# A two-layer retention, delta-rule and memory decoder: memory operands and gate columns laid out anew, and the loop over layers written out

## The chip, the cores and the metric

The kernel runs on one core of one Trainium2 chip. The metric is device time in microseconds (us) for one launch, as the median of several runs. One more execution is recorded by the hardware profiler, and all durations below come from that one. The engines are PE (matrix products; PEld is its weight load), DVE (vector), ACT (scalar functions), POOL (here it issues DMAs) and SP (it issues the weight DMAs).

## The reference

Two decoder layers run over 256 prompt tokens and 8 sample tokens, 264 columns in all, in float32. Per layer:

```
h = x + 1/2 * post(SwiGLU_1(pre(x)))                               D_MODEL 1024, D_FF 2816
h = h + post(W_out( sum_i sigmoid(gate_i) * W_branch_i(branch_i(pre(h))) ))
h = h + 1/2 * post(SwiGLU_2(pre(h)))
branches: retention (4 heads), gated delta rule (4 heads), cross-attention into 256 memory rows
memory keys and values:  mem_k = rms_norm(mem, norm_mem[l]) @ w_mem_k[l],  the same for mem_v
gated delta rule:        a, b = 8 columns of xn @ w_in;  g = -exp(a_log) * softplus(a + dt_bias);  beta = sigmoid(b)
```

Only the gain `norm_mem[l]` differs between the layers in the input of the memory products; the 256 memory rows themselves are the same. The post norms need sums of squares over the features.

## The kernel before, in words

**Layout and precision.** Activations lie transposed: features on the 128 partitions, in 8 tiles, and the 264 tokens as columns. Every large product is made of three products in the 32-bit reduced format (fp32r): high part times high part, input low part times weight high part, input high part times weight low part. So each chunk of weights that arrives in `raw` (two slots of 2048 columns, up to 1 MB each) is split by ACT into its high part (`wh`, L1178) and by DVE into the remainder (`wl`, L1596). Small products (sums of squares over partitions, transposes, decays, the 8 gate columns) are full float32 products, which the chip runs as two records of matmul each.

**Stages.** The table `PHASES` gives the order of the weight groups of a layer: mvb (memory values, second half), f1i and f1o (first SwiGLU), mk (memory keys), mq, rqk, rv (queries, retention), gq, x2, rg, x0, gz, g1 (delta rule, and the branches with their gates), b1 (delta branch's output), out, mva (memory values of the next layer, first half), f2i, f2o (second SwiGLU). A group is 48 matmuls on PE (33 in f1o and f2o). While PE is in group n, SP loads group n+2 or n+3, and ACT and DVE split group n+2. The small work of the branches hangs between the groups, written by hand: functions `after`, `mid` and `inner` on PE, and their counterparts on ACT and DVE. Each engine runs its own program; semaphores alone tie them, and within an engine the order is the written one.

**The loop over layers.** Every engine holds one copy of a layer inside `Fori(0, L)` with L = 2, and the layer number `l` is a register. A wait for "the nth use in layer l" is then a register sum followed by a wait. Inside it the long stages f1i, f1o, f2i and f2o are inner loops of four groups a turn.

**The memory rows.** The prologue makes the transposed, normalised rows in `y`, scales them by the first layer's gain into `memh` (ACT, L1252) and `meml` (DVE, L1688), and stores the unscaled rows to DRAM (`mem_t`, 1 MB). `memh` and `meml` share their place with the hidden units and with `old` of the delta branch, so they are made anew in every layer: POOL loads the rows into `mnt` (L531) after `o_gdn`, ACT scales them after group 0 of stage out, and DVE makes four of eight remainders after group 0 and four after group 1 of out. Stage out is followed by the total `p2` (L648), by mva and by the norm of the residual (`n3`, L641).

**The gates.** `gab` multiplies the 8 tiles of `y` as the stationary side by 64 columns of `wab` as the moving side, 24 float32 products, after group 2 of mq (L732). Its 8 useful columns per token tile become `gb`. In x2, after group 0, `gcol` makes four products of 4 columns (L923, L924) and `gev` eight of 8 columns (L930). In x0, after group 3, `gmt` sums squares by eight products of 8 columns (L1074).

## Time and profile before

| what | value |
|---|---|
| median of 3 runs | 2129.01 us (2123.88 to 2131.65) |
| profiled execution, its own time | 2127.21 us |
| its span, first to last instruction | 2125.6 us |
| PE busy | 1990.0 us, 94% of the span, 15638 matmuls |
| DVE, ACT busy | 1325.7 us (62%), 911.0 us (43%) |
| DMA | 370.94 MB, mean 175 GB/s |
| chain that ended last | PE 74%, DVE 15%, issue 6%, ACT 3%, DMA 1% |

The profiled execution is 1.8 us under the median and inside the range of the runs. A busy PE is not a PE at its peak, because matmuls overlap; the time from one start to the next tells what one costs. The chain is followed back from the last instruction through whatever released each step, so an engine's share of it is what sets the end, and "issue" is time in which the engine waited for nothing that the profile shows.

### The profile page before, as it was taken

The numbers are of one execution on the slowest core, as the hardware profiler recorded it, in microseconds if no ns is written. First come the engines' busy times: TensorE is split into PE (matmuls) and PEld (weight loads), VectorE is DVE, ScalarE is ACT, GpSimd is POOL, SyncE is SP. The second block draws the span as 40 slices with busy tenths as digits, with TensorE's granted clock in tenths as the row PEclk, the third lists the DMA queues.
The fourth block names the chain that finished last, engine by engine and source line by source line (L and its number), as shares of the span: only waits on it lengthen the run. The fifth ranks groups of instructions, "written<-read, shape, count | busy, mean of one in ns | idle before, by whom it ended". The sixth has DMA issues, their size and how long they took to land.

```text
span 2125.6 us, 42629 instructions
## 1 busy us (share of the span) xinstructions
PE 1990.0 (94%) x15638; PEld 1937.2 (91%) x15638; DVE 1325.7 (62%) x1996; ACT 911.0 (43%) x997; POOL 118.2 (6%) x173
## 2 busy tenths in 40 slices
PE   4999999999998999899989999999999899989997
PEld 3999989899987998899989998988999899979997
DVE  3655576647547767756566556675664767776556
ACT  2444345324553454444344434452355343444433
POOL 1000001001110101000000000010111000000000
PEclk8999999999999999999999999999999999999998
DMA  6665657545653546466656655664556345536654
GB/s 214 179 178 167 189 165 224 165 155 189 216 175 100 183 154 231 140 183 177 169 159 181 182 168 159 205 222 140 188 193 208 119 141 187 179 120 178 179 165 151
DMA packets 437539, 370.94 MB, mean 175 GB/s; under 512 B 9427, under 2 KB 415317, under 8 KB 437011
## 3 DMA queue, kind: packets, MB, share of 16 engines
q1 hardware_dynamic: 413520, 280.86, 44.4%
q0 software_dynamic: 23856, 87.98, 12.5%
q8 instruction: 95, 1.56, 0.3%
q14 instruction: 68, 0.55, 0.1%
HBM read 343.16 MB, written 25.64 MB: 173 GB/s over the span
## 4 chain that ended last, share of the span: by engine, by line
PE 74%; DVE 15%; issue 6%; ACT 3%; DMA 1%; DVEq 1%; SPq 0%; ACTq 0%
PE proj L607 47%; PE proj L630 4%; PE proj L625 4%; PE proj L626 4%; PE proj L605 2%; PE aux L817 2%; DVE wl L1596 1%; PE aux L657 1%; PE aux L902 1%; DVE y L1735 1%; PE aux L1029 1%; DVE c_t L2044 1%; DVE t_t L2138 1%; DVE qkvt L1907 1%; PE aux L748 1%
## 5 line engine op out<-in xcount | busy, mean ns | idle before, releaser
L1596 DVE TENSOR_TENSOR wl<-raw,wh 128x2048 fp32r<-128x2048 f32 (+1 forms) x284 | 608.3, 2142 | 196.1 <-ACT wh L1178 170.9
L1178 ACT CAST wh<-raw 128x2048 fp32r<-128x2048 f32 (+1 forms) x284 | 507.5, 1787 | 429.1 <-PE proj L607 263.7
L607 PE MATMUL proj<-xh,wh 128*128 128x264 f32 x2688 | 418.8, 293 | 4.7 <-ACTq L1270 4.5
L607 PE MATMUL proj<-xl,wh 128*128 128x264 f32 x2688 | 419.6, 291 | 1.4 <-DVEq L1708 1.4
L607 PE MATMUL proj<-xh,wl 128*128 128x264 f32 x2688 | 406.1, 288 | 3.7 <-DVE wl L1596 3.6
L607 PEld LDWEIGHTS proj<-xh,wh 128*128 128x128 f32 x2688 | 357.6, 190 | 11.7 <-ACTq L1270 5.0
L607 PEld LDWEIGHTS proj<-xl,wh 128*128 128x128 f32 x2688 | 361.6, 191 | 2.7 <-DVEq L1708 2.6
L607 PEld LDWEIGHTS proj<-xh,wl 128*128 128x128 f32 x2688 | 356.2, 190 | 5.4 <-DVE wl L1596 5.4
L626 PE MATMUL proj<-hl,wh 128*128 128x264 f32 x704 | 174.5, 284 | 0.0
L625 PE MATMUL proj<-hh,wh 128*128 128x264 f32 x704 | 174.4, 285 | 0.0
L626 PEld LDWEIGHTS proj<-hl,wh 128*128 128x128 f32 x704 | 132.7, 188 | 0.0
L625 PEld LDWEIGHTS proj<-hh,wh 128*128 128x128 f32 x704 | 132.5, 188 | 0.0
L1630 DVE TENSOR_TENSOR tmpf<-proj,gate 128x264 f32<-128x264 f32 x88 | 38.1, 432 | 141.4 <-PE proj L607 141.4
L817 PE MATMUL aux<-pv,sring 128*128 128x64 f32 x512 | 86.4, 250 | 12.1 <-DVEq L360 12.1
L630 PE MATMUL proj<-hh,wl 128*128 128x264 f32 x704 | 96.4, 285 | 0.0
L817 PEld LDWEIGHTS aux<-pv,sring 128*128 128x128 f32 x512 | 80.6, 192 | 13.8 <-DVEq L360 10.8
L1216 ACT ACTIVATE gate<-proj 128x264 f32<-128x264 f32 x120 | 47.0, 392 | 102.4 <-PE proj L607 101.4
L630 PEld LDWEIGHTS proj<-hh,wl 128*128 128x128 f32 x704 | 90.3, 188 | 0.0
L1245 ACT ACTIVATE sqt<-proj 128x264 f32<-128x264 f32 x48 | 18.8, 392 | 111.1 <-PE proj L630 82.2
L1383 ACT COPY full<-proj 128x256 f32<-128x256 f32 x32 | 12.0, 374 | 126.3 <-PE proj L607 126.3
L1646 DVE TENSOR_SCALAR y<-proj,gl 128x264 f32 (+1 forms) x48 | 23.6, 492 | 57.4 <-ACTq L1246 53.8
L1789 DVE CUSTOM_DVE_ANT_0 junk<-sring,aux 128x256 f32<-128x256 f32 x128 | 46.4, 417 | 14.3 <-PE aux L705 4.8
(389 smaller groups left out, 2574.7 us busy)
## 6 DMA issues: line engine op xcount, KB each, us to landing
raw<-ffn_w_in SPq DMA_DIRECT2D x176, 512.0 KB, 4.8
raw<-w_in SPq DMA_DIRECT2D x80, 1024.0 KB, 5.5
raw<-ffn_w_out SPq DMA_DIRECT2D x64, 704.0 KB, 4.5
sring<-cache_mem_k POOLq DMA_DIRECT2D x32, 512.0 KB, 5.1
sring<-cache_mem_v POOLq DMA_DIRECT2D x32, 512.0 KB, 3.9
out<-sring POOLq DMA_DIRECT2D x32, 512.0 KB, 4.5
sring<-state_gdn POOLq DMA_DIRECT2D x32, 512.0 KB, 4.9
raw<-w_mem_v SPq DMA_DIRECT2D x12, 1024.0 KB, 5.2
```

Source lines behind the costliest of these rows:

```text
L605: mm = pe.matmul(o, a[:, k, t * P:(t + 1) * P], w[:, s, k * 256:(k + 1) * 256], **go)
L607: mm = pe.matmul(o, w[:, s, k * 256 + t * P:k * 256 + (t + 1) * P], a[:, k, :], **go)
L625: pe.matmul(o, w, high[:, kk, :], start=(kk == 0), stop=False)
L626: pe.matmul(o, w, low[:, kk, :], start=False, stop=False)
L630: mm = pe.matmul(o, wl[:, s, k * P:(k + 1) * P], high[:, kk, :], start=False, stop=(kk == FT - 1))
L817: mm = pe.matmul(values.o[:, 0, k * WIDE:(k + 1) * WIDE], sring[:, values.slot, k * P:(k + 1) * P], pv[:, col:col + WIDE], start=True, sto ...
L1178: act.copy(wh[:, slot, 0:size], raw[:, slot, 0:size]).then_inc(hi_done[slot], 1)
L1216: order(act.activation(gate[:, slot, :], proj[bank][:, 0:T], func))
L1596: dve.tensor_sub(wl[:, slot, 0:size], raw[:, slot, 0:size], wh[:, slot, 0:size].bitcast(F32)).then_inc(split_done[slot], 1)
L1630: order(tt(tmpf[:], proj[bank][:, 0:T], gate[:, u % 2, :], ALU.mult))
L1646: order(ts_(y[:, j, :], proj[bank][:, 0:T], gl[:, j, gain:gain + 1], None, ALU.mult))
L1789: order.apart(dve.tensor_tensor_reduce(junk[:, z, :], sring[:, slot, z * 256:(z + 1) * 256], o[:, 0, z // 2 * 256:(z // 2 + 1) * 256], 1.0 ...
```

## The change

Four things are changed.

1. **Memory operands.** The prologue makes high and low parts for both layers, the second pair in `saveh` and `savel`, and stores that pair to DRAM (`next_h`, `next_l`, 2 MB). In each layer POOL loads both straight into `memh` and `meml` (2 MB) once ACT tells `b1_done`, in group 0 of out. The scaling by ACT and DVE in stage out is gone, and so are `mnt` and `gmem`. PE waits for the load ahead of mva.
2. **Gate columns.** `wab` is split by DVE into high and low parts (`wabr`, 40 columns: 8, a gap, 8). It is now the stationary side: 16 fp32r products with 264 moving columns (`gaw`) after group 1 of mq. DVE copies the 40 rows to `tmpf`, and three float32 products against `sel` add the two halves and turn them (`gab`) after group 2.
3. **Wide products.** `gcol` is two products of 8 columns, `gev` one of 64 columns against a diagonal that DVE makes in `gus`, `gmt` two of 32 columns.
4. **The loop over layers** is a Python loop on all five engines: two copies of the layer in sequence, with waits on constants. The inner loops stay.

```diff
-            pool.wait_ge(pro_dve, 16)
-            pool.dma_start(mem_t, y[:, :, 0:NM]).then_inc(mem_saved, 16)
+            pool.wait_ge(M["mem_split"], 2)
+            pool.dma_start(next_h, saveh[:]).then_inc(mem_saved, 16)
+            pool.dma_start(next_l, savel[:]).then_inc(mem_saved, 16)
...
-            with pool.Fori(0, L) as l:          # the same on sync, tensor, scalar and vector
+            for l in range(L):
...
-                pool.wait_ge(mem_saved, 16)
-                pool.wait_ge(M["o_gdn"], l + 1)
+                pool.wait_ge(mem_saved, 32)
+                pool.wait_ge(M["b1_done"], l + 1)
                 passed(pool)
-                pool.dma_start(mnt[:], mem_t).then_inc(mem_loaded, 16)
+                pool.dma_start(memh[:], next_h).then_inc(mem_loaded, 16)
+                pool.dma_start(meml[:], next_l).then_inc(mem_loaded, 16)
...
                         if g == 1:
                             spread(0)
+                            ready("wab_split")
+                            o = begin(l, "gaw")
+                            for k in range(KT):
+                                pe.matmul(o[0:40, 0, 0:T], wabr[:, k, :], xh[:, k, :], start=(k == 0), stop=False)
+                            for k in range(KT):
+                                mm = pe.matmul(o[0:40, 0, 0:T], wabr[:, k, :], xl[:, k, :], start=False, stop=(k == KT - 1))
+                            end(mm, "gaw")
                     elif g == 2:
-                        pe.wait_ge(wab_loaded, 16 * (l + 1))
+                        ready("abx")
                         o = begin(l, "gab")
                         for t in range(3):
                             n = P if t < 2 else NS
-                            for k in range(KT):
-                                mm = pe.matmul(o[0:n, 0, t * WIDE:(t + 1) * WIDE], y[:, k, t * P:t * P + n], wab[:, 8 * k:8 * k + WIDE],
-                                               start=(k == 0), stop=(k == KT - 1))
+                            mm = pe.matmul(o[0:n, 0, t * 8:t * 8 + 8], tmpf[0:40, t * P:t * P + n], sel[0:40, :], start=True, stop=True)
...
-                        for c in range(2):
-                            pe.matmul(o[:, 0, c * 4:c * 4 + 4], tri[:], gb[:, c, 0:4], start=True, stop=True)
-                            mm = pe.matmul(o[:, 0, 8 + c * 4:12 + c * 4], ones[:], gb[:, c, 0:4], start=True, stop=True)
+                        pe.matmul(o[:, 0, 0:8].rearrange("p (c h) -> p c h", c=2), tri[:], gb[:, 0:2, 0:4], start=True, stop=True)
+                        mm = pe.matmul(o[:, 0, 8:16].rearrange("p (c h) -> p c h", c=2), ones[:], gb[:, 0:2, 0:4], start=True, stop=True)
...
-                        for h in range(H):
-                            for k in range(2):
-                                c = (k * H + h) * NS
-                                mm = pe.matmul(o[:, 0, c:c + NS], gb[0:NS, 2, k * H + h:k * H + h + 1].broadcast_to([NS, P]), ident[0:NS, 0:NS],
-                                               start=True, stop=True)
-                        end(mm, "gev")
+                        end(pe.matmul(o[:, 0, 0:2 * H * NS], ones[0:NS, :], gus[0:NS].rearrange("p c b -> p (c b)"), start=True, stop=True), "gev")
...
-                        for h in range(H):
-                            for dt in range(2):
-                                mm = pe.matmul(o[:, 0, h * NS:(h + 1) * NS], ones[:], csum[:, 2 * h + dt, :], start=(dt == 0), stop=(dt == 1))
+                        for dt in range(2):
+                            mm = pe.matmul(o[:, 0, 0:H * NS].rearrange("p (h b) -> p h b", b=NS), ones[:], csum[:, dt:KT:2, :],
+                                           start=(dt == 0), stop=(dt == 1))
...
-                pe.wait_ge(M["mem_split"], l + 2)
+                pe.wait_ge(mem_loaded, 32 * (l + 1))
                 products(l, "mva", memh, meml, "natural", groups=(0,))
...
-            scale_memory(0, y)
+            scale_memory(0, memh)
+            scale_memory(1, saveh)
...
-                def next_memory(g):
-                    if g == 0:
-                        act.wait_ge(mem_loaded, 16 * (l + 1))
-                        scale_memory((l + 1) % L, mnt)
-                stream(l, "out", squares(l), after=next_memory, hold=True)
+                stream(l, "out", squares(l), after=lambda g: tell("b1_done") if g == 0 else None, hold=True)
...
-            split_memory(1, y)
+            split_memory(0, memh, meml)
+            split_memory(1, saveh, savel)
             stream(0, "mv0")
-            dve.wait_ge(mem_saved, 16)
...
                 stream(l, "mvb", groups=(1,))
+                dve.wait_ge(mem_saved, 32)
                 stream(l, "f1i", hidden_tile(l, True))
...
+                dve.wait_ge(wab_loaded, 16 * (l + 1))
+                order(cp(wabr[:, :, 0:8], wab[:]))
+                order(tt(wabr[:, :, 32:40], wab[:], wabr[:, :, 0:8].bitcast(F32), ALU.subtract))
+                tell("wab_split")
...
+                    if g == 1:
+                        order(cp(tmpf[0:40], take(dve, l, "gaw")[0:40, 0, 0:T]))
+                        release(dve, "gaw")
+                        tell("abx")
...
+                        order(tt(gus[0:NS], gb[0:NS, 2, :].unsqueeze(2).broadcast_to([NS, 2 * H, NS]),
+                                 ident[0:NS, 0:NS].unsqueeze(1).broadcast_to([NS, 2 * H, NS]), ALU.mult))
...
-                order(cp(gmem[:], gains[:, :, bass.ds((l + 1) % L + 12, 1)]))
-                stream(l, "out", result_tile(l, 3, "sqp"), hold=True,
-                       late=lambda g: split_memory(l + 2, mnt, range(4 * g, 4 * g + 4)) if g < 2 else None)
+                stream(l, "out", result_tile(l, 3, "sqp"), hold=True)
```

Adding `gaw` to the list of small products moves the PSUM banks of the nine that follow it by one place; from `ms1` on the banks are as before.

On PE in stage mq, from the turn of the first memory keys on, the kernel before has (aux are the PSUM banks of the small products, proj those of the large ones; names in brackets are the semaphores waited for):

```order
L607 MATMUL proj<-xh,wh 128x264 [waits bank_free1]
L607 MATMUL proj<-xh,wh 128x264 x7
L607 MATMUL proj<-xl,wh 128x264 x8
L607 MATMUL proj<-xh,wl 128x264 x8
L727 REGISTER_ALU
L573 REGISTER_ALU [waits wab_loaded]
L732 MATMUL aux<-wab,y 128x64 [waits aux_free1]
L732 MATMUL aux<-wab,y 128x64 x15
L732 MATMUL aux<-wab,y 8x64 x8
L705 MATMUL aux<-qst,selr 128x256 [waits aux_free2]
```

The changed kernel has in the same stage, one group earlier and then at the same place:

```order
L707 MATMUL aux<-qst,selr 128x256
L731 MATMUL aux<-xh,wabr 40x264 [waits aux_free3,wab_split]
L731 MATMUL aux<-xh,wabr 40x264 x7
L733 MATMUL aux<-xl,wabr 40x264 x8
L609 MATMUL proj<-xh,wh 128x264 [waits bank_free0,hi_done0]
...
L609 MATMUL proj<-xh,wl 128x264 x8
L740 MATMUL aux<-sel,tmpf 128x8 [waits aux_free2,abx]
L740 MATMUL aux<-sel,tmpf 128x8
L740 MATMUL aux<-sel,tmpf 8x8
L707 MATMUL aux<-qst,selr 128x256 [waits aux_free3]
```

The 24 products after group 2 are replaced by 16 after group 1 and 3 after group 2, and the second lot waits for DVE (`abx`).

On DVE in stage out, groups 0 and 1, the kernel before has (meml are the low parts of the memory rows, wl those of the weights, acc the running sum of squares):

```order
L1596 TENSOR_TENSOR wl<-raw,wh 128x2048 [waits order_dve,hi_done0]
L1686 REGISTER_ALU
L1688 SCALAR_TENSOR_TENSOR meml<-mnt,gmem,memh 128x256 [waits memhi]
L1688 SCALAR_TENSOR_TENSOR meml<-mnt,gmem,memh 128x256 x3
L296 ISA [waits order_dve]
L1144 REGISTER_ALU
L1645 REGISTER_ALU [waits first_done]
L1646 TENSOR_SCALAR y<-proj,gl 128x264 [waits sq_ready]
L1647 TENSOR_TENSOR acc<-acc,sqt 128x264 [waits order_dve]
```

and the changed kernel:

```order
L1593 TENSOR_TENSOR wl<-raw,wh 128x2048 [waits order_dve,hi_done0]
L296 ISA
L1643 TENSOR_SCALAR y<-proj,gl 128x264 [waits sq_ready,first_done]
L1644 TENSOR_TENSOR acc<-acc,sqt 128x264 [waits order_dve]
L1643 TENSOR_SCALAR y<-proj,gl 128x264 [waits order_dve,sq_ready,group_done1]
```

The remainders are out of DVE's way, and so are the register sums ahead of each tile.

On PE at the end of the first layer the kernel before has (the branch back is at L662, the target is the first row of mvb):

```order
L648 MATMUL aux<-acc,ones 128x264 [waits aux_free0]
L662 REGISTER_ALU
L662 COMPARE_AND_BRANCH
```

and the changed kernel runs on:

```order
L650 MATMUL aux<-acc,ones 128x264 [waits aux_free0,sqp]
L607 MATMUL proj<-wh,memh 128x256 [waits bank_free0,hi_done0]
L607 MATMUL proj<-wh,memh 128x256 x7
L607 MATMUL proj<-wh,meml 128x256 x8
L607 MATMUL proj<-wl,memh 128x256 [waits split_done0]
```

The branch between the total `p3` and mvb is gone; what stands on both sides of it is the same.

## Rows read from the trace of the kernel before

**Rows 1.** Busy time by stretch: us, each engine's busy time, PEclk, DMA share, GB/s.
```profile
311.00:352.00 41.00, 41.00 (x302) 37.61 (x302) 26.52 (x77) 17.28 (x26) 5.99 (x8) 1.00 0.66 212
508.00:586.00 78.00, 76.25 (x615) 75.04 (x613) 48.14 (x88) 43.77 (x40) 12.45 (x17) 0.98 0.65 207
668.00:720.00 52.00, 48.18 (x406) 47.03 (x405) 36.09 (x49) 23.69 (x31) 3.77 (x5) 1.00 0.40 129
888.00:1016.00 128.00, 128.00 (x1060) 128.00 (x1059) 75.51 (x89) 56.00 (x49) 0.00 (x0) 1.00 0.63 175
848.00:850.00 2.00, 2.00 (x19) 2.00 (x18) 1.32 (x4) 2.00 (x2) 0.00 (x0) 1.00 1.03 403
864.00:866.00 2.00, 2.00 (x11) 1.95 (x10) 1.07 (x1) 1.46 (x2) 0.00 (x0) 0.50 0.99 261
```

**Rows 2.** Chain that ended last: start, length, engine, tile, line, count.
```profile
318.16 4.51 PE aux L732 x48
516.50 1.88 PE aux L930 x16
700.07 1.92 PE aux L1074 x16
```

**Rows 3.** Timeline of mq and x2: start, length, engine, line, operation, [idle before].
```profile
314.10 0.08 DVE L1789 DVE_READ_ACCUMULATOR2_ANT sall<- 128x1 f32 x1
515.49 0.34 PE L923 MATMUL aux<-gb,tri 128*128 128x4 f32 x2
```

**Rows 4.** Timeline of the end of out, both layers.
```profile
843.15 3.31 ACT L1252 ACTIVATE memh<-mnt,gains 128x256 fp32r<-128x256 f32 x8
845.89 8.04 SPq L424 DMA_DIRECT2D raw<-w_mem_v  x2
853.23 1.67 DVE L1688 SCALAR_TENSOR_TENSOR meml<-mnt,gmem,memh 128x256 fp32r<-128x256 f32 x4
853.82 1.91 ACT L1178 CAST wh<-raw 128x2048 fp32r<-128x2048 f32 x1 [1.11 <-DMA raw<-w_mem_v]
858.25 2.29 DVE L1596 TENSOR_TENSOR wl<-raw,wh 128x2048 fp32r<-128x2048 f32 x1 [0.62 <-DVE acc L1647]
863.01 1.25 PE L648 MATMUL aux<-acc,ones 128*128 128x264 f32 x2 [4.93 <-DVEq L1651]
876.00 1.80 DVE L1733 RECIPROCAL rt<-rt 128x264 f32<-128x264 f32 x1 [1.55 <-ACTq L1270]
1892.94 1.25 PE L648 MATMUL aux<-acc,ones 128*128 128x264 f32 x2 [4.90 <-DVEq L1651]
```

**Rows 5.** Timeline of the totals p1 and p3, and of the next layer's start.
```profile
267.27 0.71 PE L648 MATMUL aux<-acc,ones 128*128 128x264 f32 x2 [1.85 <-DVEq L1651]
279.72 1.80 DVE L1733 RECIPROCAL rt<-rt 128x264 f32<-128x264 f32 x1 [1.55 <-ACTq L1270]
1079.11 0.97 PE L648 MATMUL aux<-acc,ones 128*128 128x264 f32 x2 [1.84 <-DVEq L1651]
1083.57 2.07 PE L605 MATMUL proj<-wh,memh 128*128 128x256 f32 x8 [3.49 <-issue]
1096.87 1.80 DVE L1733 RECIPROCAL rt<-rt 128x264 f32<-128x264 f32 x1 [4.32 <-ACTq L1270]
```

**Rows 6.** Chain that ended last, in stage b1 of both layers.
```profile
806.89 6.87 DMA raw<-w_branch_gdn
1837.36 6.16 DMA raw<-w_branch_gdn
```

**Rows 7.** Timeline around b1 (first two rows) and of the prologue.
```profile
804.87 0.55 POOL L531 DMA_DIRECT2D mnt<-mem_t  x1 [35.46 <-issue]
815.73 2.29 DVE L1596 TENSOR_TENSOR wl<-raw,wh 128x2048 fp32r<-128x2048 f32 x1 [2.14 <-ACT wh L1178]
51.44 2.29 DVE L1596 TENSOR_TENSOR wl<-raw,wh 128x2048 fp32r<-128x2048 f32 x1 [10.31 <-ACT wh L1178]
```

**Rows 8.** Landing times of the DMAs issued at L424, min, median, max.
```profile
DMA to landing us min/median/max: 4.2/5.1/14.5
```

More of the change, by code:

```diff
@@ L96 @@
          + ["p2", "n3", "p3"])
-ONE_BANK = ("n1 n2 n3 p1 p2 p3 gab smt spt rks gcs rqd gcol gev gqd gkS gmt mqs0 mqs1 mqs2 mqs3 "
+ONE_BANK = ("n1 n2 n3 p1 p2 p3 gaw gab smt spt rks gcs rqd gcol gev gqd gkS gmt mqs0 mqs1 mqs2 mqs3 "
             + " ".join(f"{n}{k}" for n in ("sp", "rd", "gd") for k in range(2 * NS)) + " "
@@ L127, in build @@
     (t_ident, t_swap, t_tri, t_masks, t_rot, t_dec, t_kdec, t_sel) = tables
-    mem_t = nc.dram_tensor("mem_t", (P, KT, NM), F32).ap()
+    next_h, next_l = (nc.dram_tensor(n, (P, KT, NM), F32R).ap() for n in ("next_h", "next_l"))
     ctx = ExitStack()
@@ L194, in build @@
         sqw = at("sqw", 29184, [P, KT, T])
-        mnt = at("mnt", 16896, [P, KT, NM])
+        saveh, savel = at("saveh", 0, [P, KT, NM], F32R), at("savel", 8192, [P, KT, NM], F32R)
         xnat = at("xnat", 0, [P, 3, D])
@@ L428, in _ @@
                     load(0, 0, name, PLAN[name], 0, g)
-            with sp.Fori(0, L) as l:
+            for l in range(L):
                 for name, _, _ in PHASES[1:]:
@@ L485, in store_prompt_state @@
                 pool.dma_start(to[l, 0].rearrange("h k v -> k h v"), stg[:].rearrange("p (h v) -> p h v", h=H)).then_inc(done, 16)
-            with pool.Fori(0, L) as l:
+            for l in range(L):
                 passed(pool)
-                pool.dma_start(wab[:, 0:KT * 8].rearrange("p (k n) -> p k n", n=8), w_in[l].rearrange("(k p) n -> p k n", p=P)[:, :, C_AB:C_AB + 8]).then_inc(wab_loaded, 16)
+                pool.dma_start(wab[:], w_in[l].rearrange("(k p) n -> p k n", p=P)[:, :, C_AB:C_AB + 8]).then_inc(wab_loaded, 16)
                 for n in range(SRING):
@@ L661, in _ @@
             products(0, "mv0", memh, meml, "natural")
-            with pe.Fori(0, L) as l:
+            for l in range(L):
                 def ready(name):
@@ L1247, in squares, with scale_memory @@
                 return tile
-            def scale_memory(layer, src):
+            def scale_memory(layer, out):
                 for k in range(KT):
-                    order.apart(act.activation(memh[:, k, :], src[:, k, 0:NM], ACT.Copy, scale=gains[:, k, bass.ds(layer + 12, 1)]))
+                    order.apart(act.activation(out[:, k, :], y[:, k, 0:NM], ACT.Copy, scale=gains[:, k, layer + 12:layer + 13]))
                 order.wait()
@@ L1258, in _ @@
                 split(0, s, 0, GW)
-            scale_memory(0, y)
+            scale_memory(0, memh)
+            scale_memory(1, saveh)
             order.fresh()
             stream(0, "mv0", copied(0, lambda g, t: mvn[:, t, g * 256:(g + 1) * 256]))
-            with act.Fori(0, L) as l:
+            for l in range(L):
                 def ready(name):
@@ L1562, in _ @@
             order(dve.memset(qsm[:, H * NS:], 0.0))
-            order(dve.memset(wab[:, KT * 8:], 0.0))
+            order(dve.memset(wabr[:].bitcast(F32), 0.0))
             dve.sem_inc(pro_act, 1)
@@ L1588, in _ @@
             dve.sem_inc(pro_dve, 1)
-            order(cp(gmem[:], gains[:, :, 12:13]))
             dve.sem_inc(M["x_half"], 1)
@@ L1681, in merge_tile, with split_memory @@
                 return tile
-            def split_memory(n, src, tiles=range(KT)):
-                if 0 in tiles:
-                    dve.wait_ge(M["memhi"], n)
-                for k in tiles:
-                    order.apart(stt(meml[:, k, :], src[:, k, 0:NM], gmem[:, k, :], memh[:, k, :].bitcast(F32), ALU.mult, ALU.subtract))
+            def split_memory(layer, high, low):
+                dve.wait_ge(M["memhi"], layer + 1)
+                for k in range(KT):
+                    order.apart(stt(low[:, k, :], y[:, k, 0:NM], gains[:, k, layer + 12:layer + 13], high[:, k, :].bitcast(F32), ALU.mult, ALU.subtract))
                 order.wait()
-                if KT - 1 in tiles:
-                    dve.sem_inc(M["mem_split"], 1)
+                dve.sem_inc(M["mem_split"], 1)
             order.fresh()
@@ L1695, in _ @@
                 split(0, s, 0, GW)
-            split_memory(1, y)
+            split_memory(0, memh, meml)
+            split_memory(1, saveh, savel)
             stream(0, "mv0")
-            dve.wait_ge(mem_saved, 16)
             dve.wait_ge(M["stz"], 2)
-            with dve.Fori(0, L) as l:
+            for l in range(L):
                 def ready(name):
```

14 lines of the change are left out of this document (7 added, 7 removed).

## The prediction

> **What bounds the kernel now.** I read busy time by stretch first. In mq PE is busy for all of 41.00 us, in f2i for all of 128.00 us, in x2 for 76.25 of 78.00, in x0 for 48.18 of 52.00 [rows 1]. So in most of the program PE's instruction stream is the limit, and a record taken off PE is worth its distance to the next start. The f2i stretch gives the price of a large matmul: 1060 starts in 128.00 us, 0.121 us each [rows 1]. Then I read the chain that ended last: the small products that the change shrinks stand on it, 4.51 us for the gate columns, 1.88 us for `gev`, 1.92 us for `gmt` [rows 2]. The timeline then shows the places where PE stands still: 4.93 and 4.90 us ahead of the total p2 at the end of out, waiting for DVE, where p1 and p3 wait 1.85 and 1.84 us [rows 4, 5]; and 3.49 us at the start of the second layer, waiting for nothing that the profile shows [rows 5]. Last, in b1 the chain runs through a weight DMA of 6.87 us, 6.16 us in the second layer [rows 6].
>
> **The change part by part.** The sum is made against the profiled execution's 2127.2 us.
>
> *Small products, on PE.* Gate columns: 48 records go, 4.51 us [rows 2]. In come 16 products with 264 moving columns at 0.121 us [rows 1], 1.94 us, and three float32 products, 6 records at the 0.118 us of `gev` (1.88 / 16 [rows 2]), 0.7 us. Saved: 1.87 us. `gcol`: its 8 records run from 515.49 until `gev` at 516.50, 1.0 us [rows 2, 3]; half go, 0.5 us. `gev`: 16 records become 2, with 64 columns, which take 0.094 us in L732 (4.51 / 48): 1.88 - 0.19 = 1.69 us. `gmt`: 16 records at 0.12 us become 4: 1.44 us. A wider moving side has no row of its own at 32 columns; it lies between the 4 to 8 columns of `gcol` and `gev` and the 64 of L732, and none of these is above 0.13 us. Together 5.5 us per layer, 11.0 us for two. In mq and x2 nothing else is late and it counts in full. In x0 PE idles for 3.8 us of 52 because the inversion goes back and forth between PE, ACT and DVE [rows 1], so I let a third of `gmt`'s part drown there: 10.0 us. Bounds: 5 (half is absorbed) and 11.
>
> What DVE does in addition (two small operations for `wabr`, a copy of 40 rows, one product for `gus`) lies in stages where it is busy for 26.5 of 41 us and 48 of 78 us [rows 1], so I cost it at nothing. The new wait `abx` stands behind group 2 of mq on PE, with sample scores and the next group queued behind it. DVE's last score of that turn ended at 314.10 and PE came to the gate products at 318.16 [rows 2, 3]; the copy fits into those 4 us, and PE comes 1.9 us later than today. If it did not, the price would be the wait itself, at most 2 us a layer.
>
> *Stage out.* ACT loses 3.31 us of scaling and DVE two lots of 1.67 us [rows 4]. PE ended its last product at 863.01 - 4.93 = 858.08. DVE's last split ran from 858.25 to 860.54, and from there to p2 it took 2.47 us for the last two tiles. Without the remainders that split can start when ACT's weight cast ends, 853.82 + 1.91 = 855.73, since the tiles before it are then done; it ends at 858.0 and p2 starts at 860.5: 2.5 us earlier [rows 4]. What is late next is the weight DMA that ACT waits for (1.11 us). In the second layer I take the limit that p1 shows, 1.85 us behind PE's last product: 1892.94 - 4.90 + 1.85 = 1889.9, 3.0 us earlier [rows 4, 5]. Afterwards: from p2 to the reciprocal of the next norm today's kernel takes 876.00 - 863.01 = 12.99 us, from p1 279.72 - 267.27 = 12.45 us [rows 4, 5]; after the long idle the two matmuls of the total take 1.25 instead of 0.71 us and the stretch behind it has a granted clock of 0.50, the lower level of 1.2 GHz [rows 1, 4]. A shorter idle should leave the clock up: 0.5 us each. Together 5.5 + 1.1 = 6.6 us. Bounds: 0 (the load's traffic takes it, below) and 8.
>
> PE's new wait is for the 2 MB load, with mva, the sum n3 and all of f2i queued behind it. The load can be issued when ACT has cast the weights of group 0, at about 843.2, where the scaling began [rows 4]. At the 403 GB/s of the fullest stretch [rows 1] 2 MB need 5.2 us, at half of that, sharing with weights, 10.4: it lands by 856, before PE wants it at 860.5.
>
> *Start of the second layer.* From p3 to the reciprocal it takes 1096.87 - 1079.11 = 17.76 us, where the same work behind p1 takes 12.45 [rows 5]. The 3.49 us of waiting for nothing and the slow matmuls behind it (2.07 us for eight) are the difference. Both go when PE runs straight on: 5.3 us. Bounds: 3.5, the gap alone, and 5.8.
>
> *Stage b1.* Today's 1 MB load of `mnt` is issued at 804.87, next to the weight DMA of 806.89 that the chain waits for [rows 6, 7]. That DMA took 6.87 and 6.16 us, where the median of its kind is 5.1 [rows 8]. The load moves out of this stage, so 1.8 + 1.1 = 2.9 us. DVE stood idle for 2.14 us behind it in the first layer [rows 7], so there is room. Bounds: 0 (others share the queue) and 4.
>
> *Register sums.* With constants the register operations ahead of waits go. Where PE streams they cost nothing: 128.00 of 128.00 us busy with them [rows 1]. Between DVE tiles they may be worth a few hundredths each. I take 2 us, bounds 0 and 8.
>
> *Prologue.* Eight more scalings on ACT and eight on DVE, about 3.3 us on each, fall into a stretch where DVE idles 10.31 us behind ACT [rows 7], which itself waits for PE's first memory group: nothing. If that cover were gone it would be 3.3 us. The 2 MB store goes out later than today's 1 MB; DVE waits for it before f1i, some 25 us later.
>
> Sum: 10.0 + 6.6 + 5.3 + 2.9 + 2 = 26.8 us, 2127.2 - 26.8 = 2100.4 us. The median of the runs is 1.8 us above the profiled execution, so I forecast 2102 us.
>
> The Trainium skill has a rule on the third term: "Runtime: NRT & Kernel Launch", section "Instruction fetch mechanics", says that code is fetched ahead in sequence only, and that a taken branch to code outside the window at hand stalls the engine. The trace agrees at the start of the second layer (3.49 us) and not in the inner loops, whose branches back show no gap. By the rule the four inner loops would have something to give too; by the rows they have nothing, and they stay in any case.
>
> **The rivals.**
>
> *A, products gain less.* Stages mq, x2 and x0 turn out to be tied to DVE and ACT soon after PE gets faster. For it: x0's idle 3.8 us. Against: none in mq. The products give 3 instead of 10 and the register sums nothing: 2111 us.
>
> *B, the memory load collides.* From 843 on POOL has 2 MB of memory rows and 2 MB of sample keys to load, beside the weights of mva (845.89 [rows 4]), where DMA is full already (share 1.03 [rows 1]). If the memory rows, whose pieces are 8 KB, go ahead of the weights' 1 KB pieces, the weights come later by up to 2 MB / 403 GB/s = 5.2 us in the first layer, and every us of it is a us at p2, since ACT's cast, DVE's split and the last tiles follow each other. Then the first layer loses 5.2 - 2.5 = 2.7 us instead of gaining 3.0, and the second gains nothing: 2102 + 5.7 + 3.5 = 2111 us. If also the load itself ran at the slowest rate seen, 14.5 us for 1 MB [rows 8], it would land at 872, and PE would wait 11.7 us ahead of mva in each layer: 2125 us. For it: the 14.5. Against: that one stood behind POOL's whole first batch of loads in the prologue, and the load is first in POOL's queue.
>
> *C, slower: fetching the written-out code stalls PE.* Place: the inner loops. f1i and f2i turn five times, f1o and f2o three, so there are 12 branches back in a layer, 24 in all. Should they cost what the branch at the layer's end costs, 3.49 us, because the copies lie differently in memory: 24 x 3.49 = 84 us, 2186 us. It decides from 8 of the 24 on (26.8 / 3.49). Against: none of them costs anything now, and the bodies only get shorter.
>
> *D, writing out the layers is worth more.* If each engine answers faster wherever it waited on a register, the register term is 12 instead of 2: 2092 us. For it: "issue" is 6% of the chain. Against: most of that is between operations whose waits are constants already.
>
> **How the numbers follow.** Forecast 0.58 (range of its own 2094 to 2110), A 0.14, B 0.12, C 0.04, D 0.12. The range 2089 to 2119 leaves out C, the far end of B and the ends of D. A measurement of this kernel can tell 0.5%, 10.6 us, from no change, so faster means below 2118.4. That takes the forecast, A, D and most of B, less a tenth for what I haven't seen: 0.87. Same: 0.09. Slower: 0.04, C.
>
> **What would show it.** Right: p2 follows PE's last product of out by under 3 us and the reciprocal follows p2 by 12.5; no gap on PE between p3 and mvb, and 12.5 us to the reciprocal; L731 and L733 some 2 us together, stages mq and x2 2 us shorter each; the b1 weight DMA near 5 us. Wrong: PE waiting for `mem_loaded`, `abx` or `wab_split`; ACT's cast before the last tiles of out waiting for its DMA by several us; PE gaps without a releaser in f1i or f2i.

## The result and the profile after

The changed kernel takes 2107.01 us (median of 4 runs, 2103.46 to 2107.55), the kernel before 2129.04 us (4 runs, 2123.88 to 2131.65). The ratio is 0.9896, with a 95% interval of 0.9874 to 0.9917: 22 us less, where I forecast 2102 us and 26.8 us less. The profiled execution has a span of 2105.6 us against 2125.6.

The timeline at the three totals and at the reciprocals behind them answers to [rows 4, 5] (start, length, engine, line, operation, [idle before]); the lines have moved a little: the total is L650, products with memory rows L607.

```profile
863.43 1.25 PE L650 MATMUL aux<-acc,ones 128*128 128x264 f32 x2 [12.12 <-DVEq L1648]
876.65 1.80 DVE L1728 RECIPROCAL rt<-rt 128x264 f32<-128x264 f32 x1 [1.71 <-ACTq L1272]
1078.69 0.71 PE L650 MATMUL aux<-acc,ones 128*128 128x264 f32 x2 [1.86 <-DVEq L1648]
1079.05 1.29 PE L607 MATMUL proj<-wh,memh 128*128 128x256 f32 x8
1091.27 1.80 DVE L1728 RECIPROCAL rt<-rt 128x264 f32<-128x264 f32 x1 [0.67 <-ACTq L1272]
1873.51 0.71 PE L650 MATMUL aux<-acc,ones 128*128 128x264 f32 x2 [1.85 <-DVEq L1648]
```

Two of the three places went as forecast: the second p2 follows PE's last product by 1.85 us instead of 4.90, and at the start of the second layer PE goes straight from p3 to the memory products and the reciprocal follows p3 by 12.58 us instead of 17.76. The first p2 is the opposite: PE stands still for 12.12 us, where it was 4.93 [rows 4]. The same view, of POOL, SP and ACT, shows why:

```profile
835.12 0.55 POOL L532 DMA_DIRECT2D memh<-next_h  x1 [71.18 <-issue]
835.66 0.57 POOL L533 DMA_DIRECT2D meml<-next_l  x1
836.57 0.91 POOL L490 DMA_DIRECT2D wab<-w_in  x1 [0.34 <-issue]
837.47 3.03 POOL L473 DMA_DIRECT2D sring<-cache_mem_k  x4
838.84 0.37 SPq L424 DMA_DIRECT2D raw<-w_mem_v  x1
841.00 0.58 POOL L495 DMA_DIRECT2D dec_tab<-t_dec  x1
856.75 1.90 ACT L1179 CAST wh<-raw 128x2048 fp32r<-128x2048 f32 x1 [10.80 <-DMA raw<-w_mem_v]
```

The weight group `w_mem_v` was issued at 838.84, between POOL's loads, and landed only at 856.7; the chain of waits has it as one piece:

```profile
838.84 17.89 DMA raw<-w_mem_v
```

Busy time by stretch (columns as in [rows 1]): the DMA engines are full in both stretches, and PE has nothing to do from 852 to 856.

```profile
846.00:852.00 6.00, 5.32 (x44) 5.10 (x43) 0.93 (x2) 0.00 (x0) 0.00 (x0) 1.00 1.04 355
852.00:856.00 4.00, 0.00 (x0) 0.00 (x0) 0.00 (x0) 0.00 (x0) 0.00 (x0) 0.88 1.05 369
```

In the prologue weights come late too. ACT takes the root of the first norm (L1277) behind a weight cast, and that cast waits for the weights of f1i:

```profile
67.83 1.91 ACT L1179 CAST wh<-raw 128x2048 fp32r<-128x2048 f32 x1 [4.86 <-DMA raw<-ffn_w_in]
70.33 1.80 DVE L1728 RECIPROCAL rt<-rt 128x264 f32<-128x264 f32 x1 [9.18 <-ACTq L1272]
```

To see the whole program at once I aligned the 284 weight splits of DVE (`wl<-raw,wh`) of both kernels, one by one, and took the distance between the first splits of two stages as the length of a stage. Beside it stands an estimate of what the clock cost in it, half of the time at granted clock 0.50 (less where PE stands still meanwhile). DVE splits about two groups ahead of PE, so on PE each stage here begins with the last two groups of the stage before.

| stage | before, layer 1 / 2 | after, layer 1 / 2 | clock cost before | after |
|---|---|---|---|---|
| start to f1i | 70.17 / - | 75.88 / - | | |
| f1o | 66.83 / 66.81 | 68.16 / 66.37 | 0 / 0 | 0 / 0 |
| mq | 31.25 / 31.01 | 29.15 / 28.33 | 0 / 0 | 0 / 0 |
| gq | 100.29 / 100.22 | 96.44 / 97.39 | 3.4 / 3.4 | 0 / 1.7 |
| x2 | 76.99 / 76.98 | 73.59 / 74.27 | 1.7 / 1.7 | 0 / 0 |
| x0 | 97.20 / 97.18 | 95.40 / 95.04 | 3.4 / 3.4 | 3.4 / 3.4 |
| b1 | 23.59 / 22.89 | 22.14 / 21.94 | 0 / 0 | 0 / 0 |
| out and mva | 53.58 / 54.04 | 61.13 / 50.19 | 5.1 / 5.1 | 8.5 / 1.7 |
| mvb, between the layers | 27.07 | 21.76 | 5.1 | 0 |

### The profile page after: what moved, and what is told of

Read it like the earlier page. It is cut to its first block, busy times and chain, and to the rows that moved or that the text cites. A ratio compares the mean times of both kernels' runs of the same rounds, so it can differ in the third digit from the quotient of the medians.

```text
span 2105.6 us, 40642 instructions
## 1 busy us (share of the span) xinstructions
PE 1972.0 (94%) x15526; PEld 1918.5 (91%) x15526; DVE 1323.2 (63%) x1993; ACT 908.0 (43%) x989; POOL 119.7 (6%) x176
## 4 chain that ended last, share of the span: by engine, by line
PE 73%; DVE 15%; issue 5%; ACT 4%; DMA 2%; SPq 0%; DVEq 0%; ACTq 0%
PE proj L609 47%; PE proj L632 4%; PE proj L627 4%; PE proj L628 4%; PE aux L824 2%; DVE wl L1593 2%; PE aux L659 1%; ACT wh L1179 1%; PE aux L909 1%; DVE y L1730 1%; PE aux L1030 1%; DMA raw<-w_mem_v 1%; PE proj L607 1%; DVE qkvt L1914 1%; DVE c_t L2051 1%
## 5 line engine op out<-in xcount | busy, mean ns | idle before, releaser
L824 PEld LDWEIGHTS aux<-pv,sring 128*128 128x128 f32 x512 | 79.8, 190 | 12.2 <-DVEq L360 12.2
```

What stands on the lines that cost most here:

```text
L824: mm = pe.matmul(values.o[:, 0, k * WIDE:(k + 1) * WIDE], sring[:, values.slot, k * P:(k + 1) * P], pv[:, col:col + WIDE], start=True, sto ...
```

## The experiments

The kernels were timed at four different times, each time beside the kernel before, whose median was 2128.0 to 2129.6 us. The ratios below are each to that one, and two kernels of different times are best compared by their ratios.

**Layers written out, nothing else** (`loops_only`). On the kernel before, the same for the five engines:

```
-            with sp.Fori(0, L) as l:
+            for l in range(L):
```

> The kernel before with nothing but its two layers written out on all five engines. Forecast of the terms: 5.3 us at the start of the second layer (no gap between p3 and the next product, 12.5 us from p3 to the reciprocal) and 2 us for register sums: 2129.0 - 7.3 = 2121.7 us, everything else as before (p2 behind an idle time of 4.9 us, the memory scaling in out). Rival D (engines answer faster at every wait): 12 us of register sums, 2112 us. Rival: the written-out code costs fetches in the inner loops: gaps without a releaser on PE in f1i or f2i, slower than 2124 us.

Measured: 2111.42 us (2108.94 to 2114.75), ratio 0.9914 (0.9899 to 0.9928), 18 us less. The start of the second layer gave its 5.5 us (27.07 to 21.60), and rival D was right about the size of the rest. DVE's part of the inversion in x0, before and here:

```profile
672.92 0.69 DVE L2044 TENSOR_TENSOR c_t<-a_t,masks 128x512 f32<-128x512 f32 x1
673.74 0.69 DVE L2138 TENSOR_TENSOR t_t<-t_t,aux 128x512 f32<-128x512 f32 x1
674.74 0.69 DVE L2044 TENSOR_TENSOR c_t<-a_t,masks 128x512 f32<-128x512 f32 x1 [0.31 <-DVE t_t L2138]
690.17 1.66 DVE L1971 SCALAR_TENSOR_TENSOR sring<-sring,egb,aux 128x256 f32<-128x256 f32 x4 [0.68 <-DVE gdb L1922]
```

```profile
667.59 0.69 DVE L2044 TENSOR_TENSOR c_t<-a_t,masks 128x512 f32<-128x512 f32 x1
668.32 0.69 DVE L2138 TENSOR_TENSOR t_t<-t_t,aux 128x512 f32<-128x512 f32 x1
669.25 0.69 DVE L2044 TENSOR_TENSOR c_t<-a_t,masks 128x512 f32<-128x512 f32 x1 [0.24 <-DVE t_t L2138]
684.05 1.66 DVE L1971 SCALAR_TENSOR_TENSOR sring<-sring,egb,aux 128x256 f32<-128x256 f32 x4 [0.23 <-DVE gdb L1922]
```

Each step comes 0.07 to 0.09 us sooner, the update of `sring` 0.45 us. PE's idle time falls from 11.44 to 9.09 us in the first x0, from 11.30 to 9.01 in the second, and by 0.9 and 0.65 us in gq. The stage x0 itself got no shorter by that in this profile (97.20 to 97.05 us, 97.18 to 97.10), because its clock cost rose from 3.4 to 5.1 us in both layers; gq got 1.3 and 4.1 us shorter, 3.4 of the 4.1 by the clock.

**Which engine's loop it was** (`pe_written`, `dve_act_written`, `three_written`): the same edit on PE alone, on DVE and ACT, and on these three.

> The kernel before with TensorE's program alone written out in sequence; the other engines keep their loop over the layers. Written out on all engines gave 18 us (2111.4). If PE's own branch at the end of a layer is what stops it between p3 and mvb: the gap of 3.49 us goes, and with it the slow stretch behind, 5 us, and 0 to 2 us elsewhere: 2122 to 2124 us. If the reciprocal of the second layer's first norm waited for ACT or DVE coming round their own loops, its distance from p3 stays above 15 us instead of 12.5, and the time is 2126 or more.

> The kernel before with VectorE's and ScalarE's programs written out, PE, POOL and SP in their loops. If the 12 us beyond the layer's start come from operations of DVE and ACT following each other faster (in the profile of the written-out kernel c_t to t_t take 0.73 us instead of 0.82, the update of sring starts 0.23 instead of 0.68 us behind what it follows, and PE idles 2.3 us less in each x0): PE's idle time in x0 is about 9.1 us instead of 11.4 in the first layer, in gq about 6.9 instead of 7.8, together with the clock that falls less often 7 to 12 us, 2117 to 2122 us, and the gap of 3.5 us between p3 and mvb stays. If PE's own registers are the cause: within 2 us of 2129.

> The kernel before with TensorE, VectorE and ScalarE written out together, POOL and SP still in their loops. Alone, PE gave nothing measurable (2127.8) and VectorE with ScalarE 8 us (2120.0), where all five engines gave 18 us (2111.4), so 10 us are not accounted for. If the engines' gains only count together (PE's gap of 3.5 to 5 us is replaced by the branches of the others, and the other way round), it is 2111 to 2113 us, with 12.5 us from p3 to the reciprocal. If the queues of SP and POOL (weights issued earlier, once they are written out) carry the rest, it is 2118 to 2121 us.

Measured: PE alone 2127.80 us (12 runs, 2122.30 to 2131.85), ratio 0.9999 (0.9986 to 1.0011), which is nothing. My number was wrong although the start of the layer did get 4.1 us shorter in the profile (27.07 to 22.96): PE's idle time grew in both x0, to 13.03 and 12.99 us, for a reason that no run looked for. DVE and ACT alone: 2119.97 us, ratio 0.9959 (0.9943 to 0.9976), 8 us, with the idle time in x0 at 9.22 and 8.97 us as expected and the gap on PE still there, now 5.06 us:

```profile
1075.16 2.07 PE L605 MATMUL proj<-wh,memh 128*128 128x256 f32 x8 [5.06 <-issue]
```

The three together: 2116.70 us (2112.07 to 2121.94), ratio 0.9942 (0.9926 to 0.9958), 12 us, between my two numbers; the interval overlaps with that of DVE and ACT alone, so that PE adds anything isn't shown. From there to the five engines it is 5 us more (these intervals touch as well), which the runs don't locate; in the profiled executions 3.1 us, 1.6 of them ahead of f1i. The Trainium skill's "Runtime: NRT & Kernel Launch", section "Instruction fetch mechanics", has a taken branch outside the window at hand stall the engine that takes it. The trace agrees as to where: PE has the gap in the three kernels in which it loops (3.49 us before, 5.06 in `dve_act_written`, 5.39 in `products_only`) and in none in which it is written out; DVE has 1.04 us before and 1.11 in `pe_written` ahead of the copies of the second layer's gains, and nothing there in `dve_act_written`. In each of the three gaps on PE the profile has one transfer of 0.02 MB on its instruction queue (q8), and none at that place in `loops_only` and the changed kernel. That PE waits for it isn't shown, for `pe_written` has one there too and no gap on PE. Nor does the gap's length follow from what else was written out, since `products_only`, with every loop in place, has the longest.

**The small products alone** (`products_only`). On the kernel before, the gate columns and `gcol`, `gev`, `gmt` as in the change, the loop kept.

```
+                            for k in range(KT):
+                                pe.matmul(o[0:40, 0, 0:T], wabr[:, k, :], xh[:, k, :], ...
-                                mm = pe.matmul(o[0:n, 0, t * WIDE:(t + 1) * WIDE], y[:, k, ...], wab[:, 8 * k:8 * k + WIDE], ...
```

> The kernel before with the gate columns as stationary side and the wider products of gcol, gev and gmt, the layers still in a loop, the memory part as before. Forecast of the term: 10.0 us, bounds 5 and 11: 2129.3 - 10.0 = 2119.3 us. Rival A (3 us): 2126 us. If the lengths of mq, x2 and x0 in the profiled execution of the changed kernel hold (2.1, 2.5, 1.8 and 2.7, 2.5, 2.1 us less), 13.7 us: 2115.6 us. The start of the second layer keeps its gap of about 3.5 us ahead of mvb.

Measured: 2120.48 us (2116.79 to 2121.71), ratio 0.9960 (0.9946 to 0.9973), 8.5 us with bounds of 5.7 and 11.5. The forecast term holds, the 13.7 us read off the changed kernel do not: part of what mq, x2 and x0 lost there was not the products (x2 of the first layer also lost 1.7 us of clock cost).

**The memory part taken back** (`memory_undone`). On the changed kernel:

```
-            scale_memory(0, memh)
-            scale_memory(1, saveh)
+            scale_memory(0, y)
...
-                pool.dma_start(memh[:], next_h).then_inc(mem_loaded, 16)
-                pool.dma_start(meml[:], next_l).then_inc(mem_loaded, 16)
+                pool.dma_start(mnt[:], mem_t).then_inc(mem_loaded, 16)
```

> The changed kernel with its memory part taken back (one 1 MB store and load of the unscaled rows, scaling and splitting inside out, as before), so only written-out layers and the wider small products are left. If the memory part gains as forecast (6.6 + 2.9 us), taking it back costs 9.5 us: 2107.0 + 9.5 = 2116.5 us. If it loses (5.3 us in the prologue and 7.4 us at the first p2 against 3.4 us at the second and 2.4 us in b1), taking it back gains 7 us: 2100 us. From the other side: layers written out alone gave 2111.4, less 10 to 13.7 us for the products gives 2098 to 2101.

Measured: 2102.03 us (2100.31 to 2104.41), ratio 0.9879 (0.9864 to 0.9894). Without its memory part the change is 5 us faster than with it by the medians and 3.6 us by the ratios, whose intervals overlap (0.9896, 0.9874 to 0.9917, with it). So the part that I had priced at a gain of 9.5 us gives none, for that would have made 2116.5 us; that it costs some 5 fits the stages of the profile, but is not clear of the noise. Against `loops_only` it is 9.4 us, the products' share once more.

**What took the DMA engines** (`next_held`, `first_held`, `both_held`). POOL issues the gate-column load, four 512 KB loads of keys and two tables in one go, 3.1 MB. On the changed kernel they are held back until the first norm of the layer is done:

```
             for l in range(L):
+                if l:                     # next_held; first_held: if not l; both_held: always
+                    pool.wait_ge(M["xn1"], 2 * (l + 1))
```

> One wait is added to the changed kernel: in the second layer POOL issues its gate-column load, its four 512 KB key loads and its two tables only when the first norm of that layer is done (xn1). Theory 1 (these loads took the DMA engines from the weights of mva): w_mem_v lands within 6 us instead of 17.9, PE waits 1.9 to 2.5 us ahead of p2 in the first layer instead of 12.12, and the stretch from the weights of out to those of mva takes 27 us as in the second layer instead of 37.6: 10.6 us less, 2107.0 - 10.6 = 2096.4 us. Theory 2 (the 2 MB of memory rows issued just before are the cause, as rival B had it): w_mem_v still lands after 12 us or more, and the time stays within 2 us of 2107. Theory 3 (held loads hurt where they now go out, beside the first weights of f1i): 10.6 us less at p2 but a new DMA wait of 2 to 5 us at the start of f1i, 2098 to 2101 us.

> The same wait in the first layer alone: the gate-column load, four key loads and two tables of the prologue go out after the first norm. Theory 1 (in the prologue too these loads, which now start later, take the DMA engines from the first weights of f1i): ACT's cast ahead of f1i waits under 1 us for its DMA instead of 4.86, and the weights of f1i are split at 70 us instead of 75.9: 5.3 us less, 2107.0 - 5.3 = 2101.7 us. Theory 2 (the 16 scalings and splits of the second layer's memory rows set the delay): the f1i split stays at 75 us or later, and the time stays at 2107. Theory 3 (the 2 MB store of the scaled rows takes the engines): as theory 2 in time, but ACT's cast still waits for its DMA.

> Both waits. If the two losses are what theory 1 says of each, they add up: 2107.0 - 10.6 - 5.3 = 2091.1 us. If one cause is wrong, its share is missing: 2096.4 or 2101.7 us. If a shift of half a microsecond is given back by the clock elsewhere (in the profiled runs the granted clock falls for 3.4 us at other places in the two kernels, at 1.7 us each), the sum is off by up to 4 us either way.

Measured: `next_held` 2102.26 us, ratio 0.9871 (0.9854 to 0.9887). `w_mem_v` lands within 6.9 us, and p2 of the first layer follows PE's last product by 1.85 us: theory 2 falls, the memory rows alone do PE no harm. The second layer of the changed kernel says the same: there the 2 MB go out with nothing behind them, and p2 follows the last product by 1.85 us. But f1i of the second layer is 10 us longer (136.2 instead of 126.3): theory 3 was right in kind and too small. There the loads meet the weights of f1i:

```profile
1093.31 3.03 POOL L473 DMA_DIRECT2D sring<-cache_mem_k  x4
1112.12 1.90 ACT L1181 CAST wh<-raw 128x2048 fp32r<-128x2048 f32 x1 [13.55 <-DMA raw<-ffn_w_in]
1114.15 2.12 PE L611 MATMUL proj<-xh,wh 128*128 128x264 f32 x8 [7.31 <-ACT wh L1181]
```

`first_held` takes 2112.64 us (2108.20 to 2116.48), 6 us more than the changed kernel where I expected 5 less. The split ahead of f1i does come at 70.34 instead of 75.88, so the loads were the cause there too, but f1i is 136.0 instead of 126.3 us long. `both_held` has both and takes 2109.51 us (2102.99 to 2112.06), where I expected 2091.1. Held back, the 3.1 MB (4.1 with the store of `mvn`) cost 8 to 10 us in f1i of either layer; behind the memory rows they cost about 10 at the first p2, and in the prologue 5.7. Going out in one go is not enough for that: before the change the batch left at 837.74, 8.2 us ahead of `w_mem_v`, and ACT waited 1.11 us [rows 4].

**One load at a time** (`chained`, `early_spread`, `early_chained`). `chained` leaves POOL's loads at the end of the first layer where they are, and waits for each before the next:

```
                     unit(l, n)
+                    if l:
+                        pool.wait_ge(unit_loaded[n], 16 * (l * (NUNIT // SRING) + 1))
```

(the same between the two memory loads and the two tables). `early_spread` issues the prologue's loads ahead of the store of the scaled rows, and the second layer's during f1i:

```
+            pool.wait_ge(pro_dve, 16)
+            first_loads(0)
             pool.wait_ge(M["mem_split"], 2)
             pool.dma_start(next_h, saveh[:]).then_inc(mem_saved, 16)
...
+                        g = 3 + 3 * n
+                        pool.wait_ge(split_done[g % 2], use(l, PLAN["f1i"], g // 4, g % 4) + 2)
```

`early_chained` has the first of these edits, and of `chained` the waits between keys and tables.

> The changed kernel with POOL's loads where they are at the end of the first layer, but each issued only when the one before has landed (memory rows too), so that one transfer of POOL is outstanding at a time. Theory (the number outstanding sets the share that the weights are left with): w_mem_v lands within 11 us instead of 17.9, PE's idle time ahead of p2 is 2 to 6 us instead of 12.12, 2107.0 - 7 = 2100 us. Rival (bytes decide: 5 MB of POOL's loads and 2 MB of weights have to pass in any order): still 10 us or more ahead of p2, 2106 us. The prologue keeps its 5 us loss in both.

> The changed kernel with POOL's first loads of each layer (gate columns, four 512 KB of keys, two tables) put elsewhere: in the prologue ahead of the 2 MB store (after the transposes, as before the change), in the second layer one by one during f1i, each released by the split of every third weight group. Theory (what cost 10 us was 4 to 5 MB outstanding at once on POOL's queue beside a weight load that the chain needs): no DMA wait of ACT over 2 us ahead of f1i in the prologue, at the first p2 or in f1i of the second layer; 5.3 us less in the prologue and 10 us less at p2, about 2107.0 - 15.3 = 2091.7 us. Rival (any further traffic in f1i delays its weights, since these have 5.75 us per MB and no more than two buffers): each of the six loads costs 1 to 2 us in f1i, 2098 to 2104 us.

> The changed kernel with POOL's first loads of the prologue ahead of the store of the scaled rows, and those for the second layer left in place but issued one at a time, each when the one before has landed (the memory rows both at once, as in the changed kernel). By the two runs that had one of these each (early_spread 2093.0, chained 2098.6 with the 5 us loss of the prologue): p2 of the first layer within 3 us of PE's last product, f1i of the first layer 4 us earlier than in chained, 2094 us, with 2092 to 2096 as likely. If the two 1 MB memory loads at once still delay w_mem_v, PE waits 4 us or more at p2 and it is 2097.

Measured: `chained` 2098.61 us (2090.61 to 2101.15), ratio 0.9844 (0.9825 to 0.9863); `early_spread` 2093.01 us (2092.23 to 2094.55), ratio 0.9835 (0.9821 to 0.9848); `early_chained` 2092.06 us (2089.91 to 2097.09), ratio 0.9830 (0.9809 to 0.9852). The last two are 14 to 15 us faster than the changed kernel, and the fastest here. What the queue of POOL (q0) and that of SP (q1) carried while both had work, in packets, MB and share of the 16 engines' time: in the changed kernel from 840 to 844 and from 850 to 856,

```profile
q0 software_dynamic: 243, 1.28, 88.8%
q1 hardware_dynamic: 107, 0.11, 13.3%
```

```profile
q0 software_dynamic: 336, 1.20, 52.8%
q1 hardware_dynamic: 1003, 1.01, 51.2%
```

and in `chained` from 843 to 848, with the landing times of its two `w_mem_v`:

```profile
q1 hardware_dynamic: 1040, 1.05, 65.7%
q0 software_dynamic: 96, 0.66, 35.0%
DMA to landing us min/median/max: 4.9/5.0/5.0
```

With one load of POOL outstanding the weights land in 5.0 us although the memory loads of 1 MB run beside them, and p2 comes 1.85 us behind the last product. So it was neither the memory rows nor the sum of the bytes, but what POOL had outstanding while the weights were under way. Whether the number of its loads counts or their MB these runs don't separate: the two go together (5.1 MB in nine loads 17.9 us, 2.5 MB in four 9.3 us in `early_chained`, 2 MB in two 6.9 us in `next_held`, 1 MB at a time 5.0), and in `chained` the keys start at 852.47, when the weights that p2 needs have landed. In `early_spread` f1i of the second layer is 126.95 us long, 0.7 more than in the changed kernel, so six loads spaced out cost together less than one of them was feared to. In `early_chained`, where both memory loads and a load of keys can be outstanding, PE waits 3.39 us at the first p2.

## Why the prediction came out as it did

**Small products: right.** 10.0 us forecast; 8.5 in the loop, 9.4 written out, and bounds of 5 and 11 hold both. The rows agree with the working: the gate products of the first layer, whose sum I put at 2.64 us,

```profile
317.90 1.15 PE L731 MATMUL aux<-xh,wabr 128*40 128x264 f32 x8
318.89 1.12 PE L733 MATMUL aux<-xl,wabr 128*40 128x264 f32 x8
326.58 0.74 PE L740 MATMUL aux<-sel,tmpf 40*128 40x8 f32 x6
516.51 0.43 PE L933 MATMUL aux<-gus,ones 8*128 8x64 f32 x2
696.46 0.60 PE L1074 MATMUL aux<-csum,ones 128*128 128x32 f32 x4 [0.59 <-DVEq L360]
```

take 2.7 (the first three rows); PE waits for neither `abx` nor `wab_split`; `gmt` takes 0.60 instead of the 0.48 that 4 records at 0.12 us would give. Rival A falls.

**Start of the second layer: right.** 5.3 us forecast, 5.3 in the changed kernel, 5.5 in `loops_only`.

**Register sums: the step that was too small.** I took 2 us, a few hundredths at each of some hand-overs, and gave the 12 us of rival D a chance of 0.12. `loops_only` gave 18 us, 13 of them outside the layer's start, and the bound of 8 failed as well. The hundredths were right, but x0 and gq consist of such steps: they go back and forth between PE, DVE and ACT, so that PE's idle time shrinks by each. `dve_act_written` shows 8 us of it. Not all of the 13 us is register sums: in the profiled execution 10.4 us lie outside the layer's start, and the clock cost, by the estimate of the table, fell by 5.1 us there. The reasoning "PE is busy for all of f2i" [rows 1] held only for stages that were not in question.

**The clock: a term that was missing.** I counted the clock only behind the long waits. It also falls behind short ones: twice in each gq, for 3.4 us, and costs 1.7 us each time. Gq of the first layer, of the kernel before and of the changed one (busy times, granted clock third from the end):

```profile
401.80:410.70 8.90, 8.86 (x57) 8.65 (x58) 4.80 (x8) 2.30 (x2) 0.00 (x0) 0.81 0.39 122
410.70:424.50 13.80, 11.87 (x90) 11.65 (x89) 7.71 (x15) 3.15 (x6) 1.06 (x2) 0.88 0.37 122
```

```profile
406.30:413.60 7.30, 7.27 (x57) 7.12 (x58) 4.80 (x7) 2.30 (x2) 0.00 (x0) 1.00 0.46 144
413.60:425.60 12.00, 10.15 (x88) 9.93 (x87) 7.72 (x14) 3.03 (x6) 1.06 (x2) 1.00 0.49 139
```

PE does the same work in both and stood idle for 1.71 us ahead of the first stretch before the change, for 1.53 after it. Summed over all stages, those not shown too, the clock cost of the weight-split table is 37.6 us before and 26.0 after. Of the difference, some belongs to the layer's start (5.1) and is in the terms; the rest goes along with shorter waits. Which wait makes it fall isn't predictable from here: in `memory_undone` the same place in gq lost 1.7 us, in `loops_only` 3.4.

**Stage out: right in the second layer, wrong in the first; rival B happened.** The second layer gained 3.9 us over out and mva, forecast 3.5 with the clock. The first lost 7.6. The step that failed is the one on the 2 MB load (issued at about 843.2, landed by 856, ahead of PE). The load was issued at 835.12 and landed by 843.4, and PE never waited for it. What came late were the weights behind it, as B had it, but by more than B's near end of 5.2 us. B named the keys as well, but its price counts the 2 MB of memory rows alone; POOL issued 5.1 MB in one go. The weights were not issued earlier against PE's work: 12.2 us ahead of PE's last product of out before (858.08 - 845.89 [rows 4]), 12.5 us after (851.31 - 838.84). What moved is POOL's batch. Before the change it began at

```profile
837.74 0.91 POOL L489 DMA_DIRECT2D wab<-w_in  x1 [32.32 <-issue]
```

8.2 us ahead of the weights; now it stands behind the 2 MB on POOL's queue, which wait for `b1_done`, and begins at 836.57, 2.3 us ahead of them. The Trainium skill's rule that is told in the prediction ("DMA: Bandwidth & Descriptors", section "Queues, rings and completion order") is that each DMA engine goes round the queues packet by packet. What the prediction works out from it agrees in direction: from 834 to 860 the transfers in the trace average 4.5 KB on POOL's queue and 1 KB on SP's, and from 840 to 844 POOL moved 1.28 MB against 0.11. But the size of the pieces alone doesn't decide, as `chained` shows, where the same memory loads, one at a time, moved 0.66 MB against 1.05.

**Prologue: the missing cost.** I priced the extra scalings at nothing, rightly as far as the runs show (ACT is idle for 5.72 us behind them in `early_spread`), and asked of the later store only whether DVE would wait for it. I did not ask what stood behind it on POOL's queue: the 3.1 MB batch moved from 31 us to 46 us, in front of f1i's weights, and the first split of f1i came 5.7 us later. With the batch ahead of the store it was 2.0 (`early_spread`) and 0.75 (`early_chained`).

**Stage b1: right in number, half of it by luck.** 2.9 us forecast, 1.45 + 0.95 = 2.4 in the stage. The second layer bears the working out: its weight DMA takes 4.69 to 5.15 us in the seven profiled kernels without the `mnt` load there, and 6.16 to 7.75 in the seven with it. The first does not: the changed kernel has 5.68 us, but the six others without that load have 6.67 to 7.19, as long as those with it (6.16 to 7.28), and their stage is 23.1 to 23.7 us long, against 23.59 before. So the load of `mnt` was not what held that DMA; what does, no run looked for. The chain has, in `next_held`, in both layers:

```profile
793.45 6.88 DMA raw<-w_branch_gdn
1810.80 4.99 DMA raw<-w_branch_gdn
```

**The sum.** By the medians: written out 18 instead of 7.3, products 9 instead of 10, memory part -5 instead of +9.5. Together 22 instead of 26.8. The forecast came near by luck: two errors of some 11 and 14 us had opposite signs. With the loads in another order the change with its memory part is 2102.03 - 2092.06 = 10.0 us faster than without it, about what that part was priced at; but the kernel without it kept its loads where they were and waits 4.21 us at the first p2, so how much of the 10 us is the order's own isn't shown.

Left open: f1o of the first layer is 0.35 to 1.3 us longer in the kernels written out on all engines except `next_held` (0.4 shorter), with ACT waiting 2.6 to 3.8 us for a weight group of f1o; no run looked for the reason. The 5 us between `three_written` and `loops_only`, which differ in POOL's and SP's loops, aren't located either.

## What to carry to other kernels

When a step is moved, follow the queue that it stands in: list what is issued behind it and ahead of it, in MB, and which transfer of the critical chain is issued while those are outstanding; then limit what is outstanding before moving anything else. A register sum that costs 0.07 us is worth counting wherever engines hand work back and forth, for it is paid at each hand-over, even if the clock can take some of it back. A term that comes out right in number is to be checked in every run that has it: in the first b1 only one kernel of seven showed it. Test the parts of a change apart even when the sum comes out as forecast.

## What the runs showed of the hardware

- A 1 MB weight load took 17.89 us beside 5.1 MB of POOL's loads issued in one go, 9.3 beside 2.5 MB, 6.9 beside 2 MB, and 5.0 us beside one 1 MB load at a time.
- The granted clock fell for 3.4 us behind an idle time of PE of 1.71 us and did not behind 1.53 us at the same place; I do not know that the idle time decides it.
- A branch back over a layer showed a gap on the engine that took it, 3.49 to 5.39 us on PE and 1.04 to 1.11 on DVE; with PE alone written out the gap went and nothing was gained in all.
